# One-hots by one comparison for four tokens with a PSUM operand, top-k names in batches, and dots written over their row

## What is computed

```python
q = (xt @ w_pq).reshape(T, H, 2, PEER_HALF)          # H = 8 heads
s = jnp.einsum('thpd,hpkd->thpk', q, sub_keys)       # 128 keys on each of two sides
s1, i1 = lax.top_k(s[:, :, 0], K)                    # K = 16
s2, i2 = lax.top_k(s[:, :, 1], K)
cand = (s1[..., :, None] + s2[..., None, :]).reshape(T, H, K * K)
cand_idx = (i1[..., :, None] * PEER_N_KEYS + i2[..., None, :]).reshape(T, H, K * K)
top_s, pos = lax.top_k(cand, K)
idx = jnp.take_along_axis(cand_idx, pos, axis=-1)    # 128 experts per token, of 16384
g = jax.nn.softmax(top_s, axis=-1)
a = gelu(jnp.einsum('cd,ced->ce', xb, u_tab[idx])) * g
y = jnp.einsum('ce,ced->cd', a, v_tab[idx])
```

## Time and profile before

| | us |
|---|---|
| median of 3 runs (3454.69 to 3463.78) | 3459.11 |
| the profiled execution | 3475.62 |
| its span | 3474.0 |
| TensorE matmul busy | 3085.9 (89%) |
| VectorE busy | 2711.0 (78%) |
| ScalarE busy | 987.2 (28%) |
| GpSimd busy | 1418.4 (41%) |

### The profile page before, as it was taken

One profiled execution on the slowest core, in us unless ns is written; L12 is line 12 of the kernel. 1 busy time (PEld: TensorE's weight loads), 2 busy tenths in 40 slices (PEclk: granted clock), 3 DMA queues, 4 the chain that ended last, 5 costly groups with the idle time before them and its releaser, 6 DMA issues. The chain is left out here.

```text
span 3474.0 us, 43072 instructions
## 1 busy us (share of the span) xinstructions
PE 3085.9 (89%) x15866; PEld 2757.8 (79%) x15866; DVE 2711.0 (78%) x5430; ACT 987.2 (28%) x1565; POOL 1418.4 (41%) x878
## 2 busy tenths in 40 slices
PE   8997989989987888888888888866999999999997
PEld 6886877879887888787878888865787888787886
DVE  4125764559999989989899897546888898888889
ACT  2103331112222332333323333332332333333331
POOL 4113210025543333333333333335665656566563
PEclk9998999999998999999999999988999999999999
DMA  4214222336654554554555545658888788787873
GB/s 163 98 61 151 90 72 82 98 115 210 217 206 174 202 191 177 202 204 174 214 190 188 207 176 208 228 193 284 298 283 302 266 284 289 266 296 270 295 272 115
DMA packets 294042, 695.59 MB, mean 200 GB/s; under 512 B 20448, under 2 KB 136544, under 8 KB 290656
## 3 DMA queue, kind: packets, MB, share of 16 engines
q1 hardware_dynamic: 190944, 316.66, 27.8%
q0 software_dynamic: 73728, 268.47, 20.9%
q10 hardware_dynamic: 29184, 108.01, 7.9%
HBM read 565.13 MB, written 127.93 MB: 200 GB/s over the span
## 5 line engine op out<-in xcount | busy, mean ns | idle before, releaser
L787 POOL TENSOR_TENSOR u_lo<-u_raw,u_hi 128x1024 fp32r<-128x1024 f32 x128 | 321.6, 2512 | 1116.9 <-ACT u_hi L783 1116.7
L1062 PE MATMUL z_ps<-hT_hi,u_hi 128*128 128x384 f32 x2048 | 728.0, 355 | 35.2 <-POOL u_lo L787 23.8
L1063 PE MATMUL z_ps<-hT_lo,u_hi 128*128 128x384 f32 x2048 | 709.2, 346 | 0.0
L1064 PE MATMUL z_ps<-hT_hi,u_lo 128*128 128x384 f32 x2048 | 707.4, 345 | 0.0
L1346 PE MATMUL y_ps<-v_hi,a_hi 128*128 128x512 f32 x1536 | 603.8, 393 | 70.4 <-DVE a_lo L1447 45.0
L1347 PE MATMUL y_ps<-v_lo,a_hi 128*128 128x512 f32 x1536 | 601.2, 391 | 0.0
L1348 PE MATMUL y_ps<-v_hi,a_lo 128*128 128x512 f32 x1536 | 600.7, 391 | 0.0
L1397 POOL TENSOR_TENSOR v_lo<-room,v_hi 128x1024 fp32r<-128x1024 f32 x128 | 344.2, 2690 | 248.8 <-ACT v_hi L1374 247.1
L1062 PEld LDWEIGHTS z_ps<-hT_hi,u_hi 128*128 128x128 f32 x2048 | 406.4, 198 | 39.6 <-POOL u_lo L787 28.0
L1072 PE MATMUL g_ps<-hot_g,hot 128*128 128x128 f32 x1536 | 232.9, 299 | 193.8 <-DVE hot_g L1213 193.8
L1063 PEld LDWEIGHTS z_ps<-hT_lo,u_hi 128*128 128x128 f32 x2048 | 404.8, 198 | 0.0
(11 more groups left out here) (184 smaller groups left out, 5010.4 us busy)
## 6 DMA issues: line engine op xcount, KB each, us to landing
u_raw<-in_uT SPq DMA_DIRECT2D x128, 512.0 KB, 3.6
room<-in_v SPq DMA_DIRECT2D x128, 512.0 KB, 6.7
z<-z_sb ACTq DMA_DIRECT2D x128, 384.0 KB, 2.6
gates<-g_sb ACTq DMA_DIRECT2D x24, 2048.0 KB, 7.9
z_in<-z SPq DMA_DIRECT2D x16, 1536.0 KB, 12.7
g_in<-gates SPq DMA_DIRECT2D x16, 1536.0 KB, 19.5
room<-z SPq DMA_DIRECT2D x15, 1536.0 KB, 12.2
room<-gates SPq DMA_DIRECT2D x15, 1536.0 KB, 20.3
```

Of the source, the lines that this page charges most:

```text
L787: self.nc.gpsimd.tensor_tensor(self.u_lo[e][:], self.u_raw[e][:], self.u_hi[e][:].bitcast(F32), ALU.subtract).then_inc(self.u_lo_in[e], 1)
L1062: nc.tensor.matmul(o, u_hi[e][:, k], hT_hi[:, k, cols], start=(k == 0), stop=False)
L1063: nc.tensor.matmul(o, u_hi[e][:, k], hT_lo[:, k, cols], start=False, stop=False)
L1064: last = nc.tensor.matmul(o, u_lo[e][:, k], hT_hi[:, k, cols], start=False, stop=(k == KT - 1))
```

## The change

1. `make_hot` compares both sides for four tokens at once, with two 128x512 comparisons whose number table is read from PSUM (`iota_ps`). The scaling by the gate goes to ScalarE: `scale_hot(n)`, four activations of 128x128, placed between the copy of `z_half(n)` and `take_gates(n-1)`. It waits for `hot_in`; `gates(n)` now waits for `hot_g_in`.
2. Top-k: `s_cp` is dropped in `experts_in`; a head takes three slots (0 to 2 and 3 to 5), `names` runs once for four heads (slot 6 of the odd quarters), and `gaps`, Exp and `gates` run once per token block. In `score` they all come once, at its end, and VectorE's loop is written out.
3. `dot` writes its product over the row that it read.
4. The scratch of the top-k lies in the shared room; the ring of gathered rows has 3 buffers for 4.
5. SyncE waits for `found_in` ahead of the early loads in turn 7.

```diff
     def names(self, link, half):
         nc = self.nc
-        nc.vector.tensor_copy(self.top_f[:], self.top_i[:])
-        nc.vector.tensor_scalar(self.ab[:, 0], self.pos[:], 4, None, ALU.logical_shift_right)
-        link(nc.vector.tensor_scalar(self.ab[:, 1], self.pos[:], 15, None, ALU.bitwise_and))
-        link(nc.vector.tensor_copy(self.ab_f[:], self.ab[:]))
-        link(nc.vector.tensor_tensor(self.pick[:], bc(self.ab_f[:], 3, TOPK),
-                                     bc(bc(self.places[:], 1, TOPK), 1, 2), ALU.is_equal))
-        link(nc.vector.tensor_tensor(self.pick[:], self.pick[:], bc(self.top_f[:], 2, TOPK), ALU.mult))
-        link(nc.vector.tensor_reduce(self.found[:, 0:2, bass.ds(h, 1), :].rearrange("p a h k -> p a (h k)"),
+        hs = slice(half * PH // 2, (half + 1) * PH // 2)
+        nc.vector.tensor_scalar(self.ab[:, 0], self.pos[:, hs], 4, None, ALU.logical_shift_right)
+        link(nc.vector.tensor_scalar(self.ab[:, 1], self.pos[:, hs], 15, None, ALU.bitwise_and))
+        link(nc.vector.tensor_tensor(self.pick[:], bc(self.ab[:].rearrange("p a h k -> p a (h k)"), 3, TOPK),
+                                     bc(bc(self.places[:], 1, PH // 2 * TOPK), 1, 2), ALU.is_equal))
+        for a in range(2):
+            last = nc.vector.tensor_tensor(self.pick[:, a].rearrange("p (h k) c -> p h k c", k=TOPK),
+                                           self.pick[:, a].rearrange("p (h k) c -> p h k c", k=TOPK),
+                                           bc(self.top_i[:, a, hs], 2, TOPK), ALU.mult)
+        link(last)
+        link(nc.vector.tensor_reduce(self.found[:, 0:2, hs, :].rearrange("p a h k -> p a (h k)"),
                                      self.pick[:], AX.X, ALU.add))
...
-    def gates(self, link, h):
+    def gates(self, link):
         nc = self.nc
+        link(nc.vector.tensor_reduce(self.gap_sum[:], self.gap_e[:], AX.X, ALU.add))
         link(nc.vector.reciprocal(self.gap_r[:], self.gap_sum[:]))
-        link(nc.vector.tensor_scalar(self.found[:, 2, bass.ds(h, 1), :].rearrange("p h k -> p (h k)"),
-                                     self.gap_e[:], self.gap_r[:], None, ALU.mult))
+        link(nc.vector.tensor_tensor(self.found[:, 2], self.gap_e[:], bc(self.gap_r[:], 2, TOPK), ALU.mult))
...
-                v.wait_ge(places_here, 16)
-                turns(v, PH, turn)
-                finish_top(PH - 1)
+                v.wait_ge(places_here, 16)
+                for h in range(PH):
+                    turn(h)
+                tk.gaps().then_inc(gaps, 1)
+                for half in range(2):
+                    tk.names(link, half)
+                v.wait_ge(exps, 1)
+                tk.gates(link)
...
-    RING = 4
+    RING = 3
...
-        product = ctx.enter_context(nc.psum_tensor("product", [P, D], F32))
+        near = ctx.enter_context(nc.psum_tensor("near", [P, 512], F32))
+        iota_ps, iT_ps, gT_ps = near[:, 0:NK], near[:, P:3 * P].rearrange("p (a t) -> p a t", a=2), near[:, 3 * P:]
...
                     n = m - Q * (TB - 1)
+                    if n == 0:
+                        sp.wait_ge(found_in, TB - 1)
...
                 def gates(gm, n):
                     g = n % 2
-                    pe.wait_ge(hot_in[g], 4 * gm + n // 2 + 1)
+                    pe.wait_ge(hot_g_in[g], 4 * gm + n // 2 + 1)
...
+                def scale_hot(gm, n):
+                    g, t0 = n % 2, gm % Q * GT + 4 * n
+                    act.wait_ge(hot_in[g], 4 * gm + n // 2 + 1)
+                    for t in range(4):
+                        last = nc.scalar.activation(hot1_g[g][:, t], hot1[g][:, t], ACT.Copy,
+                                                    scale=gT[:, t0 + t:t0 + t + 1])
+                    last.then_inc(hot_g_in[g], 1)
...
-                            if s < TB - 1 and n % 4 == 3:
-                                act.wait_ge(gaps, 2 * m + j + 1)
+                            if s < TB - 1 and q == Q - 1 and n == 6:
+                                act.wait_ge(gaps, s + 1)
                                 tk.exp().then_inc(exps, 1)
                             if s >= GB:
+                                scale_hot(gm, n)
                                 if n:
                                     take_gates(gm, n - 1)
...
+                def top_piece(s, q, n):
+                    m, j, piece = s * Q + q, n // 3, n % 3
+                    if j < 2:
+                        h = 2 * q + j
+                        if piece == 0:
+                            v.wait_ge(s_here[j], 16 * (m + 1))
+                            tk.side(link, 0, h, s_in[j][:, 0])
+                        elif piece == 1:
+                            tk.side(link, 1, h, s_in[j][:, 1])
+                            nc.vector.engine_nop().then_inc(s_taken[j], 1)
+                        else:
+                            tk.pairs(link, h)
+                            if h == PH - 1:
+                                tk.gaps().then_inc(gaps, 1)
+                    elif n == 6 and q % 2:
+                        tk.names(link, q // 2)
+                    elif n == 7 and q == Q - 1:
+                        v.wait_ge(exps, s + 1)
+                        tk.gates(link)
...
-                    nc.vector.tensor_tensor(hot2[g][:], bc(iota[:], 1, 4), bc(iT[:, 1, t0:t0 + 4], 2, NK), ALU.is_equal)
-                    for t in range(4):
-                        last = nc.vector.tensor_scalar(hot1_g[g][:, t], iota[:], iT[:, 0, t0 + t:t0 + t + 1],
-                                                       gT[:, t0 + t:t0 + t + 1], ALU.is_equal, ALU.mult)
+                    for hot, side in ((hot2, 1), (hot1, 0)):
+                        last = nc.vector.tensor_tensor(hot[g][:], bc(iota_ps, 1, 4), bc(iT[:, side, t0:t0 + 4], 2, NK),
+                                                       ALU.is_equal)
                     last.then_inc(hot_in[g], 1)
...
-                    nc.vector.tensor_tensor_reduce(product[:], rows_in[r][:], h_own[:, b], 1.0, 0.0, ALU.mult, ALU.add,
+                    nc.vector.tensor_tensor_reduce(rows_in[r][:], rows_in[r][:], h_own[:, b], 1.0, 0.0, ALU.mult, ALU.add,
                                                    ahead.z_rows[:, b, slot:slot + 1]).then_inc(row_used, 1)
```

More of the change, by code:

```diff
@@ L700, with __init__ @@
 class TopK:
-    def __init__(self, nc, ctx):
+    def __init__(self, nc, ctx, room):
         sb = memory(nc, ctx)[0]
@@ L725, in top16, with side, pairs @@
         link(nc.vector.max_index(index[:, 8:16], out[:, 8:16], left))
[L727 to L731 removed]
+    def side(self, link, p, h, scores):
+        self.top16(link, scores, self.s_left[:, p], self.top[:, p], self.top_i[:, p, h])
+    def pairs(self, link, h):
         nc = self.nc
         link(nc.vector.tensor_tensor(self.cand[:], bc(self.top[:, 0], 2, TOPK), bc(self.top[:, 1], 1, TOPK), ALU.add))
[L735 removed]
+        self.top16(link, self.cand[:].rearrange("p a b -> p (a b)"), self.cand_left[:], self.best[:, h], self.pos[:, h])
@@ L891, in turn @@
                     query(h, 0)
-                    if not (isinstance(h, int) and h == 0):
-                        act.wait_ge(gaps, h)
-                        tk.exp().then_inc(exps, 1)
                     if not last:
@@ L912, in _ @@
                 tiles.hi(0)
-                act.wait_ge(gaps, PH)
+                act.wait_ge(gaps, 1)
                 tk.exp().then_inc(exps, 1)
@@ L940, in scores @@
                                           s_ps[p][1][:].rearrange("p (t k) -> p t k", k=NK)).then_inc(s_dve, 1)
-                def finish_top(h):
-                    tk.names(link, h)
-                    v.wait_ge(exps, h + 1)
-                    tk.gates(link, h)
                 def turn(h):
-                    last = isinstance(h, int) and h == PH - 1
+                    last = h == PH - 1
                     query(h, 0)
@@ L952, in turn @@
                         split_w(h + 1, 0)
-                    if not (isinstance(h, int) and h == 0):
-                        finish_top(h - 1)
                     scores(h, 0)
@@ L962, in turn @@
                     nc.vector.engine_nop().then_inc(s_taken, 1)
-                    tk.side(link, 0)
-                    tk.side(link, 1)
-                    tk.pairs(link)
-                    tk.gaps().then_inc(gaps, 1)
+                    for p in range(2):
+                        tk.side(link, p, h, tk.s_cp[:, p])
+                    tk.pairs(link, h)
                     chain.restart()
@@ L993, in experts_in @@
         hot2 = [sb(f"hot2_{g}", [P, 4, NK]) for g in range(2)]
+        hot1 = [sb(f"hot1_{g}", [P, 4, NK]) for g in range(2)]
         hot1_g = [sb(f"hot1_g{g}", [P, 4, NK]) for g in range(2)]
@@ L1009, in experts_in @@
         hot_in = [sem(f"hot_in{g}") for g in range(2)]
+        hot_g_in = [sem(f"hot_g_in{g}") for g in range(2)]
         g_done = [sem(f"g_done{g}") for g in range(2)]
@@ L1189, in keep_picked @@
                     nc.vector.engine_nop().then_inc(picked_in, 1)
```

(22 more changed lines are left out.)

35 lines of the change are left out of this document (18 added, 17 removed).

## The result

The changed kernel is slower: 3582.24 us (median of 4 runs, 3576.14 to 3590.02) against 3459.48 for the kernel before beside it. The ratio is 1.0356, with a 95% interval of 1.0332 to 1.0381. The forecast was 3551, between 3440 and 3625.

A forecast was written before the change was run, and what follows sets the result against it. VectorE was taken to set the pace through turn 6 before; after, a closed round through a landing. Turns 2 to 7 +119, turns 0 and 1 -40, end of `score` +12.5: +92 on 3459.1, so 3551 us, range 3440 to 3625.

The forecast's parts named there:

- the round: In turns 2 to 7, waits from `u_lo` through gather, landing and scaling to the next `u_lo`: 9.08 us plus landing per pair.
- Rival A: VectorE was the bound, so its saving is paid out: turns 2 to 7 at 43.5 us a quarter, 3219 us; chance 0.06.
- the scaling: Four 128x128 activations on ScalarE in each pair of slots: 0.9 us taken, between 0.5 and 1.25 if none overlaps.
- `u_lo` to the end of the gather: Term for each pair of slots, from `u_lo` start to the even gather's end: 3.61 us.
- `take_gates` to the next `u_lo`: Term for each pair of slots, from `take_gates` start to the next `u_lo` start: 2.08 us.
- The landings: Gather end to the waiting `dot`'s start in turns 2 to 6: 4.85 us for slots 0 and 2, 4.0 for 4 and 6.
- Turn 7: The turn without top-k: 228 us forecast, where 191 stood before.
- the end of `score`: Batched `names` and gates at the block's end, with nothing to hide them: 12.5 us more (11 to 14).
- Turns 0 and 1: No one-hots, so no new wait; VectorE falls and TensorE's floor decides: 40 us less, at least 30, at most 44.
- The ring of 3: Three row buffers cost nothing, since the buffer a gather needs was freed a pair of slots before.
- Rival D: The comparison with a PSUM operand is still held up by `u_lo`: 24 us more, 3575 us; chance 0.06.
- TensorE's clock: Half clock for 1 to 4 us after idling makes TensorE's pair of slots 12 us at most, below 13 to 14.

The follow-up runs named there:

- Experiment 4: Kernel before with only the scaling moved to ScalarE, one-hot comparisons from SBUF; old top-k and ring of 4 kept: 3616.75 us.
- experiment 9: Kernel after the change with only GpSimd's order altered, the gather ahead of `u_lo` at even slots: 3281.89 us.
- experiment 12: Kernel after the change with gathers of 2 KB per row instead of 4 and `dot` over 512 columns, so other results: 3431.28 us, one run.
- experiment 8: Kernel of experiment 7 with the gather ahead of `u_lo` at even slots; the fastest: 3256.32 us.
- experiment 7: Kernel after with `u_hi` right behind its tile's second z copy, names of two heads at a time, and a ring of 4: 3374.34 us.
- experiment 2: Kernel before with only `u_hi` moved right behind the copy of its tile's second half of z: 3443.48 us.
- experiment 6: Kernel after with `u_hi` right behind its tile's second z copy, plus a ring of 4 and one-hots scaled in place: 3399.41 us.
- experiment 10: Kernel before with only the gather moved ahead of `u_lo` at even slots: 3382.01 us.
- experiment 3: Kernel after with one-hots made and scaled on VectorE as before; batched top-k, ring of 3 and `dot` over its row kept: 3429.87 us.

## Why the prediction was right

**The mechanism.** `scale_hot(2k+1)` waits, `take_gates` and `u_hi` queue behind it, `u_lo` and the even gather behind them, and the landing closes the round. Experiment 4 shows that the moved scaling alone brings turns of 235 us, experiment 9 that the loss leaves with the gather's place in GpSimd's queue while ScalarE's wait stays, and experiment 12 that the landing is a term of the round. Rival A, VectorE's saving paid out, is what the kernel comes near to in experiments 8 and 9 (3256 and 3282, where A had 3219); in the kernel after it didn't happen. (I gave no source for A's 43.5 us a quarter, and eight slots of 5.05 are 40.4; experiment 8 reaches 45.9.)

**The mis-sized term is the scaling.** I took 0.9 us for four; the next ScalarE instruction starts 1.19 us after the first of them (1429.06 to 1430.25), near the end of 1.25 "if none overlaps". One of them alone:

```profile
L1119 ACT ACTIVATE hot_g<-hot,gT x768: 384/387/405, 1044.4 to 2437.2; 128x128 f32<-128x128 f32 x192
```

387 ns, where I had interpolated 0.31, and each next starts 0.30 after the last. The 0.29 us more in each round is 1.16 a quarter, or 23 of the 27 us that turns 2 to 6 took over the forecast. I had put the value in the middle because the size lay near the small row (16 elements). But 128 elements take 387 ns and 1024 take 1.09 us: if the two forms cost alike, some 0.29 us of each doesn't depend on the size (an estimate from these two rows), and the upper bound was nearer.

The other terms were off by less. Averaged over the 20 quarters of turns 2 to 6 (us a quarter, measured and forecast): `u_lo` to the end of the gather 14.8 and 15.4 (with the 1.0 for slot 5), landings with the batch of `names` 19.4 and 18.6, `dot` to the end of the comparison 9.7 and 9.7, `take_gates` to the next `u_lo` 10.3 and 9.6. Together these are 0.8 us a quarter more than forecast. (Summed in this way a quarter is 59.1 us, by the `iT` copies it is 58.7, so the parts are no better than to 0.4.) The batch took 8.3 us in the kernel after, for the 7.4 I had reckoned.

The median is 31 us over the forecast: +27 from turns 2 to 6, +7 from turns 0 and 1, -3, -5 and -17 from the other rows of the table, and +22 since the two profiled executions lie on different sides of their medians, which I couldn't know for the second.

**The landings** were forecast at 4.85 for slots 0 and 2 and 4.0 for 4 and 6, 17.7 us a quarter; they came at 18.3 (slot 6 by the ten quarters in which its `dot` waits at all). The split between slots was off more than the sum, so that the sum came out is partly luck.

**Turn 7** came out at +32 for +37, **the end of `score`** at +9.3 for +12.5: VectorE's tail is the 15.8 us forecast (740.70 to 756.50), but `score` itself ended 3.3 us sooner.

**Turns 0 and 1** gave 33.4 for 40. I had counted on both waits going, and TensorE's 10 us for `found_in` stayed (10.0 for the earlier trace rows's 10.7). In experiment 8 it falls to 2.3 and the two turns take 275.2, 7.7 less than in experiment 7; so this wait is most likely the missing part.

The reason I gave for the gain, VectorE's saving, is not shown. VectorE is still busy for 251 of 290 us, 125 a turn where I had 110, and experiment 2 takes the same 34 us off the kernel before with VectorE's work as it was. What the two share is that TensorE no longer waits for `u_lo`: there `u_hi` moved out from behind the Exps, and the change has one Exp for a token block instead of eight. The forecast of these turns was right for a reason that I had not seen.

**The ring of 3** at nothing: right, by experiment 6, though GpSimd does wait for it.

**Rival D** fell. The comparison from PSUM was never held up:

```profile
L1232 DVE TENSOR_TENSOR hot<-near,iT x384: 676/683/692, 1043.1 to 2431.3; 128x512 f32<-128x512 f32 x192
```

Its longest is 692 ns and its shortest 676, where the earlier trace rows had a mean of 987. Those that ran beside a `u_lo` are no exception. The second of this pair did, since `u_lo` starts at 1418.22 in the round above:

```profile
1417.76 1.28 DVE L1232 TENSOR_TENSOR hot<-near,iT 128x512 f32<-128x512 f32 x2
```

The Trainium skill, page "SBUF — State Buffer", section "Who interferes with whom", has a VectorE instruction with two SBUF inputs contend with a GpSimd instruction that reads SBUF, and one with at most one SBUF input, outside the 2-port modes, not contend. This row agrees, and so does the 1204 ns of the SBUF form in experiment 4. (The price I gave this rival was 4 us too high: turn 7 has no `names`, so 10 odd quarters are held and not 12.)

**TensorE's clock.** I had the half clock last 1 to 4 us after an idle time. That was misread. After the wait that ends at 1113.32 TensorE works another 5.4 us at the half clock, and after the other such waits in turns 2 to 6 it is 2.8 to 6.2. My bound of 12 us for TensorE's pair of slots should have been about 13.2 (10.1 and half of 6.2, an estimate), which is no longer clearly below the round. It did no harm: TensorE waited for the scaling all the same, 310.6 us.

**What I had not seen:** how much lay in the order of GpSimd's two instructions, for the kernel before as well (79 us in experiment 10). I had traced the gather behind `u_lo` as a term of the round and left it at that, and had written that VectorE sets the pace through turn 6, where 10 us of each turn hung on that order.

## What to carry to other kernels

Moving work to an idle engine adds a wait to that engine's queue: list what stands behind it, and follow that list until it either leaves the loop or comes back to the waiting instruction. If it comes back, every latency on the way (here a DMA landing of 4.6 us) is paid in each round, and busy shares say nothing about the time. Here the better cure was not to undo the move (3430 us in experiment 3) but to take the long-latency step out of the loop: a gather that needs nothing from its neighbour, issued ahead of it, turned a loss of 123 us into a gain of 179. Of these 179, 79 are had by the kernel before too when its order is changed; the change itself is then worth 100.

## What the runs showed of the hardware

- Four activations of 128x128 in SBUF with a scale per partition: 387 ns each, one every 0.30 us, 1.19 us from the first to the next instruction.
- A 128x512 comparison with its number table in PSUM took 676 to 692 ns in all 384 cases, whether or not GpSimd's `u_lo` ran beside it; the same comparison with both operands in SBUF had means of 862 to 1204 ns in turns 2 to 6 (experiments 3 and 4) and single ones of 2.9 us. The old `tensor_scalar` form, with its two scalars from SBUF, was held up too (330 ns at best, 2418 at worst, in experiment 10).
- Halving an indirect gather of 128 rows from 512 to 256 KB took only 0.7 to 1.3 us off a landing of 4.0 to 4.9, 4.22 of 18.31 us over the four slots. If the time that goes with the bytes is proportional to them, that is 8.4 us, and the other 9.9, somewhat over half, are there at any size (an estimate).
- In turns 2 to 6 the mean granted clock of TensorE was 0.88 in the kernel after, whose `gates` waited up to 9.6 us, and 0.95 in experiment 9; for the same matmuls it was busy for 909 and 844 us. Whether any of the 239 us between the two is the clock's is not shown, since TensorE waited in both.
